# A depthwise convolution shared by two engines: in its last four steps the matrix engine adds eight taps per channel in place of twelve, VectorE the four others

## The reference

```python
C_CONV = 31                                     # taps, causal, one filter per channel
def conformer_conv(h, w1, b1, dw_w, dw_b, ln_g, ln_b, w2, b2):
    z = jax.nn.glu(h @ w1 + b1, axis=-1)        # (T, 1024) @ (1024, 2048), gated
    z = causal_dw_conv(z, dw_w) + dw_b          # z[t] = sum_d w[d] * z[t - d], d = 0..30
    z = jax.nn.silu(layer_norm(z, ln_g, ln_b))  # over the 1024 channels
    return z @ w2 + b2                          # (T, 1024) @ (1024, 1024)
```

## Time and profile before

| | |
|---|---|
| median of 3 runs | 1629.83 us (1627.28 to 1630.64) |
| the profiled execution | 1626.12 us, of which its span (first to last instruction) 1624.0 us |
| TensorE busy | 1503.7 us, 93% of the span |
| VectorE busy | 854.6 us, 53% |
| ScalarE, GpSimd busy | 353.8 us (22%), 417.5 us (26%) |
| mean granted TensorE clock | 0.976 of full |

### The profile page before, as it was taken

The page is one execution under the profiler, slowest core; times in us unless marked ns, Lnnn a source line. Parts: engine busy times, 40 slices in busy tenths (PEclk is TensorE's granted clock), DMA queues, the critical chain, the costliest instruction groups (busy, mean ns, idle before and its releaser), DMA issues.

```text
span 1624.0 us, 16879 instructions
## 1 busy us (share of the span) xinstructions
PE 1503.7 (93%) x5185; PEld 804.1 (50%) x5186; DVE 854.6 (53%) x1474; ACT 353.8 (22%) x742; POOL 417.5 (26%) x673
## 2 busy tenths in 40 slices
PE   5989999998999899999979999999899899999991
PEld 3774544446886444444434334345588544444440
DVE  2454488664324433433427898999643633443343
ACT  3210000000122233233332000012141233333333
POOL 2100000000000466656510000213000146665650
PEclk9999999999999899999999999999899999999996
DMA  9636046664234689799475454454232589679846
GB/s 340 212 119 195 26 155 196 210 203 130 105 97 177 238 237 302 235 305 305 97 210 164 122 148 120 118 135 106 79 130 78 202 304 372 187 216 295 253 98 232
DMA packets 151219, 302.44 MB, mean 186 GB/s; under 512 B 17622, under 2 KB 101682, under 8 KB 142977
## 3 DMA queue, kind: packets, MB, share of 16 engines
q1 hardware_dynamic: 121696, 222.71, 41.1%
q0 software_dynamic: 21248, 65.40, 16.0%
q10 hardware_dynamic: 8224, 13.67, 2.3%
HBM read 248.56 MB, written 53.12 MB: 186 GB/s over the span
## 4 chain that ended last, share of the span: by engine, by line
PE 72%; DVE 15%; DMA 8%; issue 2%; ACT 2%; POOL 1%; SPq 0%; DVEq 0%; POOLq 0%; ACTq 0%
PE bank L1064 20%; PE bank L1224 19%; PE bank L1143 16%; PE bank L1239 10%; DVE R L1862 6%; DVE WX L1431 3%; DMA WX<-in_moe_w_gate 2%; PE bank L1332 2%; DMA R<-xn_scratch,TCUR 2%; DMA xsum_scratch<-R,TSUM 1%; PE bank L1047 1%; PE bank L1081 1%; DVE R L1408 1%; DMA WX<-in_moe_w_down 1%; DMA xsum_scratch<-R,TCUR 1%
## 5 line engine op out<-in xcount | busy, mean ns | idle before, releaser
L1064 PE MATMUL bank<-HTR,WX 128*128 128x512 f32 x1024 | 452.9, 599 | 5.8 <-DMA WX<-in_hyb_w_in 4.8
L1224 PE MATMUL bank<-WX,R 128*128 x784 | 350.1, 600 | 12.7 <-issue 6.6
L1064 PEld LDWEIGHTS bank<-HTR,WX 128*128 128x128 f32 x1024 | 192.7, 191 | 245.2 <-issue 238.4
L1224 PEld LDWEIGHTS bank<-WX,R 128*128 128x128 f32 x784 | 146.2, 191 | 183.5 <-issue 183.3
L1862 DVE SCALAR_TENSOR_TENSOR R<-R,PT 128x512 f32<-128x512 f32 (+18 forms) x288 | 231.2, 803 | 10.2
L1143 PE MATMUL bank<-WX,R 128*128 128x256 f32 x1024 | 230.8, 384 | 2.2 <-DVE R L1408 1.1
L659 POOL DMA_INDIRECT R<-xn_scratch,TCUR x204 | 200.6, 983 | 49.7 <-issue 41.1
L1143 PEld LDWEIGHTS bank<-WX,R 128*128 128x128 f32 x1024 | 194.3, 192 | 31.8 <-issue 2.8
L1239 PE MATMUL bank<-WX,R 128*128 x408 | 185.3, 597 | 4.0 <-DVE R L1674 4.0
L794 ACT ACTIVATE R<-R,MCT 128x128 f32<-128x128 f32 x408 | 162.0, 481 | 19.6 <-DVE R L1658 19.6
L1685 DVE SCALAR_TENSOR_TENSOR R<-bank,GSLOT,HTR 128x512 f32<-128x512 f32 x51 | 38.3, 751 | 207.4 <-DMA xsum_scratch<-R,TSUM 156.4
(11 more groups left out here) (223 smaller groups left out, 1100.7 us busy)
## 6 DMA issues: line engine op xcount, KB each, us to landing
WX<-in_ada_w SPq DMA_DIRECT2D x48, 1024.0 KB, 11.8
WX<-in_moe_w_gate SPq DMA_DIRECT2D x32, 1024.0 KB, 5.6
WX<-in_moe_w_up SPq DMA_DIRECT2D x32, 1024.0 KB, 8.9
WX<-in_moe_w_down SPq DMA_DIRECT2D x32, 1024.0 KB, 13.9
WX<-in_conf_w SPq DMA_DIRECT2D x20, 1024.0 KB, 9.4
WX<-glu_scratch SPq DMA_DIRECT2D x64, 260.0 KB, 4.6
WX<-in_hyb_w_in SPq DMA_DIRECT2D x10, 1024.0 KB, 11.9
xsum_scratch<-WX ACTq DMA_DIRECT2D x8, 1024.0 KB, 5.4
```

The costliest lines, as they stand in the source:

```text
L1064: ins = pe.matmul(dst[:], lhs(k), rhs(k), start=(k == 0), stop=(k == kc - 1))
L1224: ins = pe.matmul(hid, XT[:, k, :], WXP[:, bass.ds(at, 2), k, :], start=(k == 0), stop=(k == KC - 1))
```

## The change

Round 0 of `conv_taps` (d = 9 to 12) is left out in steps 12 to 15; the round that is now first starts the sum. VectorE's `taps(n)` covers those four distances with four more `scalar_tensor_tensor` in the same steps. The transfers, the diagonal matrices (all three rounds are still built) and every semaphore stay.

```diff
+def rounds_of(n):
+
+    return MAXQ - 1 if n >= NSTEP - 4 else MAXQ
...
-                for q in range(MAXQ):
+                q0 = MAXQ - rounds_of(n)
+                for q in range(q0, MAXQ):
                     for g in range(SH):
                         ins = pe.matmul((X0, X1)[n % 2][CG * g:CG * g + CG, :], TAPW[n % 2][:, g, q, :],
                                         SHIFTED[n % 2][:, g, SH * q:SH * q + HT],
-                                        start=(q == 0), stop=(q == MAXQ - 1))
+                                        start=(q == q0), stop=(q == MAXQ - 1))
                 ins.then_inc(cv_ps, 1)
...
-                for d in range(SH * MAXQ + 1, CTAPS):
+                for d in range(SH * rounds_of(n) + 1, CTAPS):
                     t0 = 0 if h else d
                     link(dve.scalar_tensor_tensor(out=o[:, t0:HT], in0=p[:, HT * h + t0 - d:HT * h + HT - d],
                                                   scalar=tap(CTAPS - 1 - d), in1=o[:, t0:HT],
                                                   op0=ALU.mult, op1=ALU.add))
```

## The result

The changed kernel takes 1641.08 us in the median (1638.41 to 1641.31, 3 runs) against 1629.83: a ratio of 1.0077, with a 95% interval of 1.0057 to 1.0097, or 9.3 to 15.8 us slower. Timed again beside more runs of the kernel before, it gave 1640.89 against 1627.40, ratio 1.0082 (1.0064 to 1.0101). The profiled execution took 1641.31 us; its span is 1639.5 us, 15.5 more than before.

What follows compares the result with a forecast made beforehand. VectorE alone was taken to set the convolution stage's end. Extra taps 12.6, slowed taps 0.9 and clock 0.8 gave +14.3 us on a median of 1629.8: 1644 us, range 1639.5 to 1649.

Steps and rivals of the forecast that it cites:

- What bounds: Convolution stage up to `x_piece`: VectorE alone sets its end, through the 3.01 us wait for the first residual addition.
- The price of a tap: VectorE in steps 12 to 15: 0.788 us for each new instruction, 3.15 a step, 12.6 us for sixteen.
- What left TensorE: `conv_taps` in steps 12 to 15: 0.91 us less a step, 3.6 us in four, counted as nothing.
- POOL's builds: POOL's matrix builds for steps 14 and 15 each slow one VectorE tap: 0.9 us, bounds nothing to 1.7.
- The sum to x_piece: At the end of the stage, the residual addition and `x_piece` come 13.5 us later, at 1165.0.
- The waits in between: TensorE's new or longer waits ahead of `conv_taps(14)`, the second projection and `x_piece`: those before `x_piece` cost nothing themselves.
- The clock: Group (0, 2) behind `x_piece` starts at the low clock: 0.8 us more, between 1.7 less and 1.6 more.
- The total: Whole kernel: 12.6 + 0.9 + 0.8 = +14.3 us, a median of 1644.
- TensorE as the bound: Rival for the convolution stage: VectorE's lag is harmless, so -3.6 us, 1626.2; chance 3%.
- no effect: Rival for the whole kernel: no change that can be told, within 0.2% or 3.3 us; chance 2%.
- a part of the shift absorbed behind the stage: Rival: a transfer or queue does not move with VectorE, so only +4 to +10 us, about 1637; chance 5%.
- more lost to the clock: Rival: waits leave TensorE slow into group (0, 2) and beyond, +18.8 us, 1648.6; chance 10%.

Runs made afterwards that it cites:

- pe_only: Changed kernel without VectorE's four extra taps in steps 12 to 15, so TensorE's round is just left out; 1628.54 us against 1627.40 before, ratio 1.0003.
- dve_only: Kernel before with VectorE's four extra taps added in steps 12 to 15, TensorE keeping all three rounds; 1642.45 us against 1627.40, ratio 1.0090.
- last_step: Changed kernel with the change made in step 15 alone; 1628.76 us against 1627.40 for the kernel before, ratio 1.0012.
- early_add: Kernel before with VectorE's residual addition of group (0, 0) moved up behind the ninth of step 15's 18 taps; 1622.85 us against 1626.49, ratio 0.9976.
- again: The changed kernel itself, unaltered, timed again beside more runs of the kernel before; 1640.89 us against 1627.40, ratio 1.0082.

## Why the prediction was right

- **What bounds.** VectorE's order up to the first residual addition sets the stage. `pe_only` (no gain), `dve_only` (the whole loss) and `last_step` (+3.16, with loads and swish untouched) show it from three sides, and `early_add` shows that it is this one wait.
- **The price of a tap.** 0.788 us each from the earlier trace rows; `last_step` gives 3.16 for four. The 594 ns by the Trainium skill's VectorE: DVE Perf Modes, section "The TRN2 errata — SBUF-src ops pay a fixed extra latency per instruction", would have made it 2.4. The half throughput that the Trainium skill's Vector Engine (DVE) Microarchitecture Reference, section "Points that are easy to get wrong", states would have made it over 4.2 by an estimate. Neither is what this instruction does here. What left TensorE was 0.86 us a step (`conv_taps(13)` 1.93 us for 2.79), not 0.91, and was taken at nothing, as it should be.
- **POOL's builds.** Forecast two slowed taps, 0.9 us; measured 0.5 us in each of steps 12 and 13 of the changed kernel, and alone in `pe_only`, 1.02.
- **The sum to x_piece.** Forecast 13.5, measured 13.55 twice. The evictions of steps 13, 14 and 15: 3.6, 7.2, 10.4 forecast, 3.66, 7.28, 10.40 measured.
- **The waits in between.** Forecast 2 to 4 us ahead of `conv_taps(14)`, 7 ahead of the second projection, 8 ahead of `x_piece`; measured 4.06, 5.66, 7.82. The 7 was over by 1.3: `conv_taps(14)` began at the late end of its forecast and took 2.58 us for 1.9, partly at the low clock. They cost nothing of their own: `conv_taps(15)` ended 7.8 us ahead of `x_piece`, and even 16.55 us for the first two groups in `again`, for 14.08, left `x_piece` at the same 13.55.
- **The clock.** This term was mis-sized: 0.8 us forecast, +0.5 measured in one profile and -0.3 in the other. That group (0, 2) would begin at the low clock was right in both; when the clock came back varied: 4.5 us after `x_piece` began in the first profile, about 3 in the second, where the group took 8.09 us, less than the 8.7 that the prediction set as its least. The term stayed within its bounds of -1.7 to +1.6. Windows of 0.1 us put the low stretches of the kernel before at 1142.2 to 1148.9 and 1152.4 to 1155.8, a little wider than the prediction read them, which would move its term by under 0.1 us.
- **The total.** 14.3 forecast, 14.0 and 13.3 in the stage, 13.5 between medians of the larger set. The forecast median of 1644 is 3 us too high mainly because it was added to a median of three runs, 1629.83, where 17 to 23 runs gave 1626.5 to 1627.4 three times.
- **Rivals.** TensorE as the bound and no effect are excluded by `pe_only` and `again`; for a part of the shift absorbed behind the stage nothing speaks, since the rest of the span is the same (463.4 before, 463.1 and 462.3 after) within the 5 us over which it varies among the profiles; more lost to the clock did not happen.

## What to carry to other kernels

When two engines both look full, shares say nothing about which way to move work: look for the wait that ends last and see whose order stands behind it. Here TensorE held 72% of the chain, and the right trade was the other way round, 0.9 us of TensorE for 3.15 us of VectorE. What a moved instruction costs or saves depends on its step: taps added in the first steps were mostly taken up by waits, taps taken away in step 12 brought VectorE only to its next wait for TensorE, and in step 15 all of it counted. A third engine can have a share too: here the moment at which POOL ran was worth up to a microsecond. Before dividing the work differently, see whether the awaited instruction can stand earlier in its engine's order; that alone was worth about 4 us (1.8 to 6.0).

## What the runs showed of the hardware

- POOL slows a VectorE instruction that reads two tensors from SBUF (taps, 0.75 to 1.2 or 1.65 us) and not one that takes one of its two from a PSUM bank: beside the builds in the kernel before, the addition and the eviction took 0.69 and 0.74 us, as always, and the reciprocal 3.35. So a shift of a microsecond in when POOL runs changes VectorE's time with no work added. Tap 0, a `tensor_scalar` with one tensor from SBUF, is slowed too: in the kernel before 1.22 us beside POOL's centring in step 11 (at 1056.51), 0.55 in steps 12, 13 and 15. For the taps, the Trainium skill's SBUF — State Buffer, section "Who interferes with whom", says that a VectorE instruction with two SBUF inputs contends with a GpSimd instruction that reads SBUF; the rows agree.
- The granted clock, once at half (1.2 GHz), does not come back as soon as work begins, and the same work can end differently. In the first profile of the changed kernel it stayed at half through 3.64 us of matmuls between two waits (1155.3 to 1158.9) and came back to full (2.4 GHz) only after the next work had run 4.5 us. In `again` the same 3.64 us of matmuls (1159.7 to 1163.4) were followed by the full clock at 1163.8, with TensorE idle, and it fell again at 1167.2, ahead of `x_piece`. In the kernel before, too, it came back with TensorE idle, 0.5 us after `conv_taps(15)` had ended.
